# Features-first input, normed in place by a row of token factors, in a hybrid encoder layer on one core

## The reference, cut to what matters

```python
def rmsnorm(x, g):
    y = x * lax.rsqrt(jnp.mean(x * x, axis=-1, keepdims=True) + EPS)
    return y * g

def trunk(x, ...):
    h = rmsnorm(x, norm1_g)                  # (1312, 1024)
    z = h @ w_in                             # pool input u, q, k, v, o, gates
    ...
    x = x + concat([y_pool, y_mlstm]) @ w_out
    x = x + expert_choice_ffn(rmsnorm(x, norm2_g), w_router, w_gate, w_up, w_down)
    return rmsnorm(x, final_g)[:, N_META:]

def expert_choice_ffn(h, ...):               # 16 experts, each takes its top-k tokens
    gate, idx = lax.top_k(softmax(h @ w_router).T, cap)      # cap: 34 prompt + 130 sample rows
    xe = h[idx]
    ye = (silu(xe @ w_gate[e]) * (xe @ w_up[e])) @ w_down[e] * gate
    out[idx] += ye
```

## Time and profile before

| | us |
|---|---|
| median of 3 runs | 1782.64 (1779.51 to 1783.49) |
| the profiled execution | 1781.83 |
| its span in the trace | 1780.0 |
| PE busy | 1736.0 (98% of the span) |
| DVE, ACT, POOL busy | 415.7, 387.3, 297.8 |

### The profile page before, as it was taken

How to read it: one execution, slowest core, us unless ns; L and a number is a source line. 1 busy time by engine, 2 the same in 40 slices (tenths; PEclk the granted TensorE clock), 3 DMA queues, 4 the chain that set the end, 5 groups by cost and what they waited for, 6 DMA issues and landing times.

```text
span 1780.0 us, 24974 instructions
## 1 busy us (share of the span) xinstructions
PE 1736.0 (98%) x10345; PEld 1403.1 (79%) x10345; DVE 415.7 (23%) x903; ACT 387.3 (22%) x891; POOL 297.8 (17%) x328
## 2 busy tenths in 40 slices
PE   7999999999999999999899999999999999999995
PEld 4555556855555774555899999999999999999995
DVE  4471212631020560069201101011010110101104
ACT  3335334332121543445000000000000000000014
POOL 0071021520101153433000010100101001010010
PEclk9999999999999999999999999999999999999998
DMA  6110212421101445524477686976859758597585
GB/s 203 50 53 4 68 36 57 107 89 36 36 17 40 154 108 180 176 86 164 167 279 251 217 269 219 304 247 206 282 206 308 257 195 285 200 312 264 182 277 199
DMA packets 169216, 302.02 MB, mean 170 GB/s; under 512 B 11804, under 2 KB 53964, under 8 KB 169152
## 3 DMA queue, kind: packets, MB, share of 16 engines
q1 hardware_dynamic: 161904, 278.06, 45.5%
q0 software_dynamic: 7248, 23.09, 5.2%
HBM read 269.77 MB, written 31.35 MB: 169 GB/s over the span
## 4 chain that ended last, share of the span: by engine, by line
PE 94%; DVE 2%; ACT 1%; DMA 1%; issue 1%; POOL 0%; SPq 0%; DVEq 0%; POOLq 0%
PE bank L2053 32%; PE bank L2072 15%; PE bank L1827 12%; PE bank L1805 9%; PE bank L1954 8%; PE bank L1740 3%; PE bank L1775 2%; PE bank L1888 2%; PE bank L1869 1%; PE bank L1787 1%; PE bank L1784 1%; PE bank L1783 1%; PE bank L2094 1%; PE bank L2028 1%; PE bank L1907 1%
## 5 line engine op out<-in xcount | busy, mean ns | idle before, releaser
L2053 PE MATMUL bank<-arena 128*128 128x164 f32 x4096 | 581.4, 303 | 1.3 <-DVE arena L1622 1.3
L2053 PEld LDWEIGHTS bank<-arena 128*128 128x128 f32 x4096 | 573.5, 191 | 1.5 <-DVE arena L1622 1.5
L2072 PE MATMUL bank<-arena 128*128 128x164 f32 x2048 | 295.8, 303 | 0.0
L2072 PEld LDWEIGHTS bank<-arena 128*128 128x128 f32 x2048 | 286.6, 190 | 0.0
L1827 PE MATMUL bank<-arena 128*128 128x512 f32 (+1 forms) x576 | 214.1, 534 | 0.0
L1827 PEld LDWEIGHTS bank<-arena 128*128 128x128 f32 x576 | 109.8, 191 | 102.7 <-issue 92.9
L1631 DVE TENSOR_TENSOR arena<-bank,arena 128x328 f32<-128x328 f32 x64 | 32.0, 499 | 659.3 <-ACT arena L1238 659.3
L818 POOL DMA_INDIRECT residual<-arena,cur_scatter x30 | 45.1, 1503 | 692.9 <-DVE arena L1640 636.1
L1805 PE MATMUL bank<-arena 128*128 128x384 f32 x480 | 155.7, 485 | 0.0
L1238 ACT ACTIVATE arena<-bank 128x328 f32<-128x328 f32 x64 | 28.4, 443 | 563.0 <-PE bank L2053 563.0
L1954 PE MATMUL bank<-arena 128*128 128x512 f32 x320 | 146.0, 599 | 0.8 <-issue 0.8
(11 more groups left out here) (262 smaller groups left out, 1498.2 us busy)
## 6 DMA issues: line engine op xcount, KB each, us to landing
arena<-in_w_up SPq DMA_DIRECT2D x32, 2048.0 KB, 14.4
arena<-in_w_down SPq DMA_DIRECT2D x32, 2048.0 KB, 9.7
arena<-in_w_gate SPq DMA_DIRECT2D x32, 2048.0 KB, 8.1
arena<-in_w_in SPq DMA_DIRECT2D x8, 1536.0 KB, 6.6
arena<-in_x_sample SPq DMA_DIRECT2D x14, 512.0 KB, 6.4
arena<-decay_rows SPq DMA_DIRECT2D x22, 256.0 KB, 4.7
arena<-state_rows SPq DMA_DIRECT2D x44, 128.0 KB, 4.1
residual<-arena SPq DMA_DIRECT2D x11, 512.0 KB, 5.7
```

Of the source, the lines that this page charges most:

```text
L2053: last = pe.matmul(ps[2 * w + fp % 2][:, a * SLOTS:(a + 1) * SLOTS], ring[2 * (fp // 2) + w][:, k, f * P:(f + 1) * P], xeT[:, k, SIDE[side ...
L2072: last = pe.matmul(ps[4 + dp % 2][:, a * SLOTS:(a + 1) * SLOTS], ring[4 + dp // 2][:, k, dt * P:(dt + 1) * P], hidT[:, k, :], start=k == 0 ...
```

## The change

The host also hands over the input features-first (`x_features_first`, 128 partitions with 8 blocks of all tokens), the gain as a column per block (`g1c`), and the first weight block as one array with contiguous rows of 12.8 KB (`w_in_first_block`, o columns and gate columns together). SP loads each tile twice: the rows as before, for the sum of squares, and the features-first copy straight into `hT` (512 bytes in a piece). DVE writes the token factors on a diagonal (`diag` = identity times factor); PE multiplies a matrix of ones by it, which gives the factors as a row on every partition; DVE multiplies each of the 8 blocks of `hT` in place by its gain column and by that row. The 8 transposes per tile and their copies fall away. PE issues 22 unread products (`warm`) first. At the first expert, a bank holds four feature blocks of one gather, and the loads of ring slots 2 and 3 wait for the tail gather. At the end the results go back in quarters of 256 features through four banks, the last `down` quarter is copied by halves, the last norm is shared by DVE, ACT and POOL, and `FIN_AT` is denser.

```diff
                 def load_x(i):
                     if i == NT - 1:
-                        sp.wait_ge(x_clear, 1)
+                        sp.wait_ge(zeroed, 1)
                     for p0, src in x_rows[i]:
                         sp.dma_start(xin[i][p0:p0 + src.shape[0], :], src).then_inc(x_in[i], 16)
+                    sp.dma_start(hT[:, :, tile_cols(i)], x_flipped.rearrange("p (k t) -> p k t", k=KT)[:, :, tile_cols(i)]).then_inc(tile_in[i], 16)
 
                 load_x(ORDER_X[0])
-                sp.dma_start(g1b, g1[0:1, :].to_broadcast([P, D])).then_inc(params_in, 16)
+                sp.dma_start(g1c[:, :], g1[:, :]).then_inc(params_in, 16)
+                sp.dma_start(Wo[:, :, :], w_first.rearrange("p (k n) -> p k n", k=KT)).then_inc(w_slot_in[0], 16)
                 load_x(ORDER_X[1])
-                load_w(0)
-                sp.dma_start(Wo[:, :, PAIR:OGW], w_view[:, :, 3328:3344]).then_inc(gw_in, 16)
                 for i in ORDER_X[2:6]:
                     load_x(i)
-                sp.wait_ge(zeroed, 2)
+                sp.wait_ge(zeroed, 3)
...
                     read_out(sp, ("wo", NT - 1, h))
-                load_expert(2)
-                load_expert(3)
                 for s in range(2):
                     n = 16 * len(range(s, NT, 2))
                     sp.wait_ge(x2_out[s], n)
                     sp.wait_ge(t_out[s], n)
+                sp.wait_ge(tail_in, 16)
+                load_expert(2)
+                load_expert(3)
...
-        FIN_AT = ((), (), (0, 1, 2), (3, 4, 5, 6), (7, 8), (9, 10), (), ())
+        last_rms, last_ready, last_out, last_weighed = sem("last_rms"), sem("last_ready"), sem("last_out"), sem("last_weighed")
+
+        FIN_AT = ((), (), (0, 1, 2, 3, 4), (5, 6, 7), (8, 9), (10,))
+        LAST_BANKS = (7, 6, 0, 1)
...
+                pool.wait_ge(fg_in, 16)
+                for q in (2, 3):
+                    pool.wait_ge(last_sum, 2 * q + 1)
+                    pool.tensor_tensor(xg[:, 256 * q - 512:256 * q - 256], xl[:, 0, 256 * q:256 * q + 256], fgb[:, 256 * q:256 * q + 256], ALU.mult).then_inc(last_weighed, 1)
                 pool.wait_ge(y_stored, 16 * NT)
                 for blk, n in BLKS:
                     pool.wait_ge(last_ready, blk + 1)
+                    if blk == 0:
+                        pool.wait_ge(last_rms, 2)
                     pool.indirect_dma_start(out=y_all[:, :], out_offset=bass.IndirectOffsetOnAxis(ap=cur_scatter[0:n, blk, :], axis=0),
...
+                def last_result(a):
+
+                    act.wait_ge(dn_full, (NE - 1) * 4 + 4 + a)
+                    act.activation(yeT[:, 6 + a, SIDE[1]:SIDE[1] + SLOTS], ps[(5, 2)[a]][:, 0:SLOTS], ACT.Copy).then_inc(dn_done, 1)
...
+                for blk in range(2):
+                    last_square(0, blk)
+                results_pair(NE - 1, 1, 2)
+                for blk in range(2):
+                    last_square(1, blk)
+                last_result(0)
+                for blk in range(2):
+                    last_square(2, blk)
+                st.settle()
+                act.sem_inc(last_sq, 1)
+                last_result(1)
+                last_square(3, 0)
+                last_root(0)
+                last_square(3, 1)
+                act.wait_ge(last_ms, 2)
+                act.wait_ge(last_weighed, 2)
+                act.activation(xl[:, 0, 512:D], xg, ACT.Copy, scale=small[:, 72:73]).then_inc(last_rms, 1)
+                last_root(1)
...
-                        multiplied(dve, ("x", i - 2, 1))
-                    st.settle()
-                    dve.scalar_tensor_tensor(xn[i % 2], xin[ORDER_X[i]], small[:, 48 + i:49 + i], g1b, ALU.mult, ALU.mult).then_inc(xn_done, 1)
-                    if i:
-                        move_xT(i - 1)
+                        multiplied(dve, ("x", i - 2))
+                    st.settle()
+                    dve.tensor_scalar(diag[i % 2], ident[:, :], small[:, 48 + i:49 + i], None, ALU.mult).then_inc(diag_ready, 1)
+                    tile = ORDER_X[i]
+                    dve.wait_ge(tile_in[tile], 16)
+                    multiplied(dve, ("x", i))
+                    b = plan[("x", i)][0]
+                    for k in range(KT):
+                        h = hT[:, k, tile_cols(tile)]
+                        st.do(dve.scalar_tensor_tensor(h, h, g1c[:, k:k + 1], ps[b][:, 0:P], ALU.mult, ALU.mult))
+                    st.settle()
+                    dve.sem_inc(free[b], 1)
+                    dve.sem_inc(h_ready, 1)
...
+                    if m < 4:
+                        k, at, w = 4 * (m % 2), (0, P)[m // 2], (P, TAILS)[m // 2]
+                        dve.tensor_copy(xeT[:, k:k + 4, at:at + w], gathered(FIRST_BANKS[m], 4, w)).then_inc(t_done, 1)
...
+                def last_rows(q):
+
+                    c = slice(256 * q, 256 * q + 256)
+                    dve.wait_ge(o_full, 6 * PAIRS - 2 + q + 1)
+                    for blk, n in BLKS:
+                        dve.scalar_tensor_tensor(xl[0:n, blk, c], ps[LAST_BANKS[q]][0:n, 256 * blk:256 * blk + 256], gatec[0:n, blk, NE - 1:NE],
+                                                 xl[0:n, blk, c], ALU.mult, ALU.add).then_inc(last_sum, 1)
...
+                last_rows(0)
+                for i in FIN_AT[5]:
+                    normed(i)
+                last_rows(1)
+                last_rows(2)
+                last_rows(3)
+                last_sums()
+                last_reciprocal(0)
+                dve.sem_inc(last_ms, 1)
+                dve.scalar_tensor_tensor(xl[:, 0, 0:512], xl[:, 0, 0:512], small[:, 72:73], fgb[:, 0:512], ALU.mult, ALU.mult).then_inc(last_ready, 1)
+                n = SB_ROWS
+                last_reciprocal(1)
+                dve.scalar_tensor_tensor(xl[0:n, 1, :], xl[0:n, 1, :], small[0:n, 73:74], fgb[0:n, :], ALU.mult, ALU.mult).then_inc(last_ready, 1)
...
+                def warm(count, b):
+
+                    for _ in range(count):
+                        pe.matmul(ps[b][:, 0:P], ident[:, :], ident[:, :], start=True, stop=True)
+
                 pe.wait_ge(ident_done, 1)
+                warm(22, 5)
                 for i in range(NT):
-                    pe.wait_ge(xn_done, i + 1)
-                    for h in range(2):
-                        b = bank(("x", i, h))
-                        for k in range(4):
-                            c = (4 * h + k) * P
-                            last = pe.transpose(ps[b][:, k * P:(k + 1) * P], xn[i % 2][:, c:c + P], ident[:, :])
-                        last.then_inc(full[b], 1)
+                    pe.wait_ge(diag_ready, i + 1)
+                    b = bank(("x", i))
+                    pe.matmul(ps[b][:, 0:P], ones, diag[i % 2], start=True, stop=True).then_inc(full[b], 1)
...
-                    for m in range(4):
-                        to = gathered(FIRST_BANKS[m], 2, P + TAILS)
-                        for a in range(2):
-                            k = 2 * m + a
-                            last = pe.transpose(to[:, a, at:at + n], xe[0:n, blk, k * P:(k + 1) * P], ident[0:n, 0:n])
-                        if blk:
-                            last.then_inc(t_full, 1)
+                    for m in range(2):
+                        to = gathered(FIRST_BANKS[2 * blk + m], 4, n)
+                        for a in range(4):
+                            k = 4 * m + a
+                            last = pe.transpose(to[:, a, :], xe[0:n, blk, k * P:(k + 1) * P], ident[0:n, 0:n])
+                        last.then_inc(t_full, 1)
...
+                def transpose_last(q):
+
+                    pe.wait_ge(dn_done, (NE - 1) * 4 + q + 3)
+                    for a in range(2):
+                        if q == 3 and a:
+                            pe.wait_ge(dn_done, NE * 4 + 3)
+                        for blk, n in BLKS:
+                            at = (SIDE[1] + SB_ROWS, SIDE[1])[blk]
+                            to = ps[LAST_BANKS[q]][0:n, 256 * blk + a * P:256 * blk + (a + 1) * P]
+                            last = pe.transpose(to, yeT[:, 2 * q + a, at:at + n], ident[:, :])
+                    last.then_inc(o_full, 1)
+
+                pe.wait_ge(o_done, 6 * PAIRS - 1)
+                down(NE - 1, 0)
+                for m in range(1, 3):
+                    down(NE - 1, m, lambda: transpose_last(m - 1))
+                down(NE - 1, 3, lambda: transpose_last(2), True)
+                transpose_last(3)
```

134 lines of the change are left out of this document (61 added, 73 removed).

## The result

The changed kernel takes 1800.24 us (median of 4 runs, 1796.94 to 1801.96) against 1783.07 of before on the same chip; ratio 1.0099, 95% interval 1.0087 to 1.0111. The prediction was 1770.2 and faster. Ratios and intervals leave out the few runs that took far longer than those beside them, whatever the kernel (before: 1833.80, 2727.05 and 6449.38 us; expert_only: 3056.18). The profiled execution took 1796.94 us with a span of 1795.1, 15.1 more than before.

The account below looks back on a forecast made before the run. PE was taken to bound the kernel, busy nearly throughout. Savings of 5.3 (first stage), 4.1 (first expert) and 3.0 us (end) sum to 12.4: from the profiled 1781.83 to 1769.4, median 1770.2 us, range 1766.0 to 1775.5.

Parts of the forecast that it names:

- Removed: eight transposes per tile, 0.87 us on the chain. Added: one product of 128 columns, two instructions: First stage: 0.87 us removed and 0.24 added per tile, so the period shrinks by 0.63 to 5.86 us.
- I count nothing for `warm`: Start: the 22 unread products save none of the 2.3 us that the first `output_gate` loses.
- the only slower one: Rival at the first expert: the moved loads become the bound, costing more than 12.4 us, time above 1783.7; chance 0.03.
- First stage: Up to the tenth `output_gate`: 5.7 us saved by shorter periods less 0.4 for a later start, 5.3 us.
- the gap brings half clock: Start: PE, nearly idle from about 9 to 13.7 us, drops to half clock, leaving the first `output_gate` near 7.9 us.
- the bound of 3.3: First stage: DVE's eight multiplications take at most 3.3 us a tile, hidden by PE.
- First expert: At the first expert: `gate_up` starts 2.3 us earlier and full clock saves 1.8 more, together 4.1 us.
- the gathers: First expert: with slots 2 and 3 out of the way each gather lands in 4.2 us, at 858.7 and 860.25.
- the lower bound of the prediction: First expert: if gathers land no sooner and the clock falls, only the regrouped banks gain, 1.0 us.
- The clock's 1.8 us: First expert: with PE's idle time cut from about 3.4 to 1.2 us, products take 9.07 instead of 10.85 us.
- End: Last expert and tail: 0.4 us saved in PE's part and 2.6 behind the last product, 3.0; bounds 1.5 and 4.2.
- the mutual exclusion that the prediction weighed: End: two-SBUF-input DVE operations and SBUF-reading GpSimd operations block each other; POOL's products could delay DVE up to 0.7 us.

Follow-up runs that it names:

- expert_only: The kernel before with only the first expert changed (loads of slots 2 and 3 behind the gathers, banks and copies regrouped): 1780.69 us, ratio 0.9990.
- shift_before_150: The kernel before with 150 idle instructions ahead of its first transposes, loop at 8551 instead of 8401: 1796.54 us, ratio 1.0082.
- spread_after_49: The changed kernel with 49 idle instructions set one at a time between long products, loop at 8401: 1771.96 us, ratio 0.9954.
- no_warm: The changed kernel without the 22 warm products, with 136 idle instructions between products, loop at 8401: 1772.99 us, ratio 0.9946.
- end_only: The kernel before with only the end changed (quarter banks, earlier norms, result multiplied by ACT, DVE and POOL): 1778.00 us, ratio 0.9974.
- loads_ahead: The changed kernel with 49 idle instructions between products and the loads of slots 2 and 3 ahead of the gathers again: 1772.12 us, ratio 0.9945.

## Why the prediction was wrong

**The step that failed** is the costing of the removed and added PE work: "Removed: eight transposes per tile, 0.87 us on the chain. Added: one product of 128 columns, two instructions", and for the other added products "I count nothing for `warm`". They were counted by duration only. Their number also sets where everything behind them lies in PE's program, and the loop's head fell 49 places, to 48 ahead of a block's edge. That is 25.3 us in the profiled run and 28.3 between medians. The profiled run was the fastest of four, with a granted clock of 0.993 over the span where the two slowest (1801.47 and 1801.96 us) had 0.990 and 0.991, so part of the 3 us between may be clock; no profile shows where. Of the rivals none had it; the only slower one put the loss on loads, with a chance of 0.03. Shown: by moving the loop alone both kernels can be made fast or slow (49 instructions take 28 us off the changed one, 150 put 10 on the one before). The edges couldn't be read from the trace of before, but the risk could: a loop of 1683 instructions, an instruction queue whose 43 packets are just the program once, and a change of PE's instruction count ahead of the loop. The Trainium skill, "Runtime: NRT & Kernel Launch", section "Instruction fetch mechanics", gives PE room for 2048 instructions in blocks of 256, with the next block fetched ahead; eight blocks less the one fetched ahead is what fits these runs. By its rule that a taken branch out of the two pages in work forces a fetch, each return would stop in any place; the runs with 43 packets disagree, their loop returns over some 1680 instructions without a stop.

With the loop back in place the changed kernel takes 1771.96 us, inside the range of 1766.0 to 1775.5. That is in part luck, since the three terms were missed in both directions, and so were sizes inside them.

**First stage**, 5.3 predicted, 5.57 in the trace. The period was 5.84 for 5.86. The start was 1.1 us later than predicted (14.81 for 13.7), since tile 3's rows landed at 12.17 instead of 11.3; the first `output_gate` took 6.67 us instead of 7.9, and the two misses cancel by luck: with the stage of before and with the new one it took 6.2 to 8.3 us from profile to profile (5.56 in shift_before_150, where it starts at 21.51). That the gap brings half clock was right: in the changed kernel 0.50 is granted from 14 to 17 us and 1.00 from 17.2, in spread_after_49, whose `output_gate` took 7.97 us, 0.50 until 20 us. (For the kernel before, half clock there is read from the length alone, 7.88 us; its windows show 1.00 at that place.) Also right was `warm` at nothing (no_warm). DVE's eight multiplications took 2.16 us, under the bound of 3.3. What wasn't foreseen is that 1.3 us of the lead goes again: behind a wait of 1.56 us at 150 us the granted clock falls in both kernels, but for longer in the changed one (windows as above, first changed, then before):

```profile
148.00:152.00 4.00, 2.44 (x27) 2.33 (x28) 1.68 (x2) 3.60 (x11) 0.00 (x0) 0.77 0.06 5
152.00:156.00 4.00, 4.00 (x13) 2.23 (x12) 1.75 (x3) 2.28 (x5) 0.00 (x0) 0.50 0.10 7
156.00:160.00 4.00, 4.00 (x9) 1.67 (x8) 0.00 (x0) 0.00 (x0) 0.00 (x0) 0.87 0.05 3
```

```profile
152.00:156.00 4.00, 2.44 (x20) 1.73 (x18) 0.10 (x1) 2.38 (x6) 0.00 (x0) 1.00 0.06 5
156.00:160.00 4.00, 4.00 (x25) 2.56 (x26) 3.33 (x4) 2.31 (x11) 0.00 (x0) 0.73 0.07 6
160.00:164.00 4.00, 4.00 (x9) 1.64 (x9) 0.00 (x0) 0.75 (x1) 0.00 (x0) 0.85 0.12 11
```

It isn't tied to the edit alone: end_only, whose first stage is that of before, has the longer stretch too, behind the same wait of 1.56 us, and spread_after_49, with the changed stage, the shorter. Over all profiles 9 of 11 kernels with the changed stage have the longer one and 2 of 7 without; whether the edit makes it likelier stays open. end_only:

```profile
156.00:160.00 4.00, 4.00 (x12) 2.18 (x12) 2.17 (x3) 2.23 (x5) 0.00 (x0) 0.50 0.09 7
160.00:164.00 4.00, 4.00 (x8) 1.67 (x7) 0.00 (x0) 0.00 (x0) 0.00 (x0) 0.71 0.07 8
```

**First expert**, 4.1 predicted, 2.4 in the changed trace (0.7 earlier, 1.7 by the clock) and 1.8 from expert_only (0 to 3.6 by its interval). The failed term is the gathers: 4.2 us each in an empty queue was the row of a later gather and isn't what these take (first 4.65, second 5.89). The move of the two loads is worth nothing (loads_ahead). What is left is the regrouping of banks and copies, 0.97 us (PE waits 0.32 for the last copy instead of 1.29), the lower bound of the prediction. The clock's 1.8 us came in the changed trace (1.67), but it comes and goes in kernels that don't touch the expert, too. The loads themselves stayed hidden, as predicted.

**End**, 3.0 predicted, 3.5 in the traces. The tail behind the last product was 7.34 us (1780.09 to 1787.43) for 7.4. The stop at the thirteenth product was 0.35 for 0.45, and the last product was out 20.07 us after the first (1760.02 to 1780.09) for 20.6. The 7.64 us behind the second scatter were 7.67. The first scatter took 1.69 us, not 2.07, and the rows show why it may be longer than the second: it began while DVE multiplied the second block, and took as much longer as that still ran. DVE's rows, before and changed:

```profile
1768.98 1.27 DVE L1706 SCALAR_TENSOR_TENSOR arena<-arena,small 36x1024 f32<-36x1024 f32 x1
```

```profile
1784.03 1.28 DVE L1761 SCALAR_TENSOR_TENSOR arena<-arena,small 36x1024 f32<-36x1024 f32 x1
```

Before, DVE still had 1770.25 - 1769.08 = 1.17 us to go when the scatter began, and the scatter took 2.07 - 0.90 = 1.17 us longer than the second; in the changed kernel it is 0.77 and 0.79. That two scatters differ in this way fits the mutual exclusion that the prediction weighed from the Trainium skill ("SBUF — State Buffer", practical consequences); no run takes DVE's work away, so it isn't shown. POOL's products of 256 columns (0.73 and 0.72 us) don't test the rule: DVE's additions beside them read one of their two blocks from a bank of PSUM, and took 0.87 us for a pair there and 0.86 without POOL.

## What to carry to other kernels

Where an engine's program has a loop, a change of the number of instructions anywhere ahead of it is a change to the loop. Before costing such an edit, compare the packets of the instruction queue with the program's blocks, and the loop's length with what is held; afterwards look at that row and at waits on "issue" at the loop's head before looking for a cause in the edit. Idle instructions between long products cost nothing that showed here, and put the loop where it should be. Leave a margin on both sides, and don't stand one instruction behind the edge, as the kernel before did by chance: here the head could lie anywhere from 8400 to 8509 (8401, 8452 and 8501 were run), and 8397 cost 59 us.

A saving worked out from a clock that "stays up" should be weighed down or left out if a stop ahead of it remains: in these traces the same 64 products took 9.2 us in 9 of 18 kernels and 10.6 to 10.9 in the others, with the expert's edit and without it.

## What the runs showed of the hardware

- PE's instructions came in packets of 16 KB, 256 instructions. A loop of 1683 was kept when it lay between 8400 and 10191 (seven blocks), and fetched again, nine packets a turn, with its head in the block before or 41 instructions into the eighth behind.
- PE's stops at a return depend on the head's distance to the next edge: 1.2 to 1.8 us for 105 instructions, 3.6 to 3.9 for 48, 5.3 to 6.0 for 23 and 7.0 to 7.3 for 3, and half clock behind the stops of the last two on top.
- Of the nine packets one came ahead of the return and eight at it or behind. That the first is the block behind the loop's end, fetched ahead, fits their times and number; it isn't shown otherwise.
- Open: where in the eighth block the fetch of the ninth begins to hurt (6 instructions in was kept in the profiled run, with timed runs up to 1788.2; 41 was not), and why the edges lie at 8400 and not at a multiple of 256 of the compiled program, 48 further on. So an edge had to be found from a stop; the count alone doesn't give it.
- An idle instruction alone took PE about 0.1 us: between 49 and 100 of them the wait behind `warm` grew from 3.13 to 8.62 us, 0.108 each, and 150 held the first transposes of the kernel before until 18.30 us. The first 20 or so pass while PE still works on what is ahead (25 left a wait of 0.54 us), so the 0.086 us that the expectations use is too low. Between products of 400 columns they cost nothing that shows.
